# Compressed scores of both key groups by one block-diagonal product of 64 columns, issued in two halves between the last projections

## The reference, cut to what matters

```python
q_t = q.reshape(B, T, G, R, dh).transpose(0, 2, 3, 1, 4)       # dh = 64, T = 512
k_cmp = compress(kc, pe_k, w1k, w2k)                           # [B, 31, G, dh]
v_cmp = compress(vc, pe_v, w1v, w2v)
mask_c = cmp_end[None, :] <= t_idx[:, None]
s_c = jnp.einsum('bgrtd,bngd->bgrtn', q_t, k_cmp) * scale
p_c = masked_softmax(s_c, mask_c)
o_cmp = jnp.einsum('bgrtn,bngd->bgrtd', p_c, v_cmp)
...
o = g[..., 0:1] * o_cmp + g[..., 1:2] * o_slc + g[..., 2:3] * o_win
```

## Time and profile before

| what | value |
|---|---|
| median of 3 executions | 1792.61 us (1789.62 to 1793.20) |
| span of the profiled execution, first to last instruction | 1792.8 us |
| mean granted TensorE clock over the span | 0.994 of full |
| PE busy | 1768.5 us (99%) |
| POOL busy | 1180.3 us (66%) |
| DVE busy | 977.7 us (55%) |
| ACT busy | 382.7 us (21%) |
| the compressed scores on PE | 4.94 us, from 1236.35 us on |

### The profile page before, as it was taken

How to read it: one execution, slowest core, us unless ns; L and a number is a source line. 1 busy time by engine, 2 the same in 40 slices (tenths; PEclk the granted TensorE clock), 3 DMA queues, 4 the chain that set the end, 5 groups by cost and what they waited for, 6 DMA issues and landing times.

```text
span 1792.8 us, 24916 instructions
## 1 busy us (share of the span) xinstructions
PE 1768.5 (99%) x8821; PEld 1397.6 (78%) x8821; DVE 977.7 (55%) x1664; ACT 382.7 (21%) x827; POOL 1180.3 (66%) x1182
## 2 busy tenths in 40 slices
PE   8999999999999999999999999999999999999998
PEld 6888888888876788888888888878446778888887
DVE  4855345545664205465513556799874987007613
ACT  3111000012246311211100001454885110000001
POOL 4676677675665467667667668755754678668862
PEclk9999999999999999999999999999999999999999
DMA  9655465451330032455335543513000222332221
GB/s 355 216 189 172 141 212 189 150 155 62 104 94 24 24 101 92 160 170 187 123 109 190 187 129 94 127 50 95 25 24 1 94 71 94 110 100 92 97 94 47
DMA packets 245548, 212.93 MB, mean 119 GB/s; under 512 B 45985, under 2 KB 240990, under 8 KB 245470
## 3 DMA queue, kind: packets, MB, share of 16 engines
q1 hardware_dynamic: 229440, 211.18, 36.9%
q10 hardware_dynamic: 16030, 0.72, 0.5%
HBM read 209.72 MB, written 2.10 MB: 118 GB/s over the span
## 4 chain that ended last, share of the span: by engine, by line
PE 70%; POOL 13%; issue 9%; DVE 5%; DMA 1%; ACT 1%; ACTq 0%; POOLq 0%; DVEq 0%
PE ps L768 18%; PE ps L770 18%; PE ps L769 18%; POOL w_lo L697 8%; POOL w_hi L692 2%; PE ps L1376 2%; POOL w_hi L691 2%; PE ps L1387 2%; PE ps L1149 2%; PE ps L1407 2%; DMA raw<-in_ffn_w_down 1%; PE ps L1170 1%; PE ps L1158 1%; PE ps L809 1%; DVE tt L2258 0%
## 5 line engine op out<-in xcount | busy, mean ns | idle before, releaser
L697 POOL TENSOR_TENSOR w_lo<-raw,w_hi 128x512 fp32r<-128x512 f32 (+4 forms) x576 | 737.2, 1310 | 11.8
L768 PE MATMUL ps<-h_hi,w_hi 128*128 128x512 f32 x1192 | 468.1, 393 | 1.8 <-DVE h_lo L2540 1.4
L770 PE MATMUL ps<-h_hi,w_lo 128*128 128x512 f32 x1192 | 464.8, 390 | 0.0
L769 PE MATMUL ps<-h_lo,w_hi 128*128 128x512 f32 x1192 | 464.7, 390 | 0.0
L689 POOL TENSOR_TENSOR w_hi<-raw,ones 128x8 fp32r<-128x8 f32 x144 | 33.6, 233 | 450.0 <-PE ps L770 385.3
L768 PEld LDWEIGHTS ps<-h_hi,w_hi 128*128 128x128 f32 x1192 | 224.1, 188 | 54.4 <-issue 5.9
L770 PEld LDWEIGHTS ps<-h_hi,w_lo 128*128 128x128 f32 x1192 | 224.0, 188 | 47.5
L769 PEld LDWEIGHTS ps<-h_lo,w_hi 128*128 128x128 f32 x1192 | 224.1, 188 | 46.0
L768 PE MATMUL ps<-g_hi,w_hi 128*128 128x512 f32 x608 | 237.7, 391 | 0.1
L770 PE MATMUL ps<-g_hi,w_lo 128*128 128x512 f32 x608 | 236.6, 389 | 0.0
L769 PE MATMUL ps<-g_lo,w_hi 128*128 128x512 f32 x608 | 236.6, 389 | 0.0
(11 more groups left out here) (405 smaller groups left out, 2415.3 us busy)
## 6 DMA issues: line engine op xcount, KB each, us to landing
ada<-in_ada_w SPq DMA_DIRECT2D x31, 1024.0 KB, 7.0
ada<-in_w_ada SPq DMA_DIRECT2D x24, 1024.0 KB, 7.0
raw<-in_ffn_w_gate SPq DMA_DIRECT2D x22, 1024.0 KB, 5.2
raw<-in_ffn_w_up SPq DMA_DIRECT2D x22, 1024.0 KB, 5.1
raw<-in_w_in SPq DMA_DIRECT2D x16, 1024.0 KB, 5.1
raw<-in_w_up SPq DMA_DIRECT2D x16, 1024.0 KB, 5.3
raw<-in_w_down SPq DMA_DIRECT2D x16, 1024.0 KB, 4.7
raw<-in_ffn_w_down SPq DMA_DIRECT2D x16, 768.0 KB, 4.7
```

The lines of the kernel that those rows point to most:

```text
L697: last = pool.tensor_tensor(lo[:, c], src[:, c], hi[:, c].bitcast(F32), ALU.subtract)
L768: pe.matmul(o, wh, xh, start=start, stop=False)
L769: pe.matmul(o, wh, xl, start=False, stop=False)
L770: return pe.matmul(o, wl, xh, start=False, stop=stop)
```

## The change

The 32 score products of 64 rows by 32 columns (one for each head and each 128 tokens; the two groups in alternation, to banks 4 and 6) are replaced by 16 products of 128 rows by 64 columns: the queries of head hh of both groups, against a `kcmp` that is now zero outside its two diagonal blocks. Half of them (tokens 0 to 255) are issued in the middle of `proj(W_QD[1], 0)`, after `hidden_turn(1)`, to bank 4; the other half between `proj(W_QD[1], 0)` and `proj(W_QD[1], 1)`, to bank 6. Each half raises `cm_s` by one. `kcmp` is cleared once, early on DVE, and then filled by two copies of 64 x 32 in place of one of 128 x 64. `cmp_scores(b)` waits for its own half and reads it from one bank.

```diff
@@ -1356,16 +1356,23 @@
         proj(W_QD[0], 0, lambda: hidden_turn(0))
         proj(W_QD[0], 1, small_keys)
         compress(1)
-        pe.wait_ge(cm_kv_ev, 1)
-        for qc in range(NQ):
-            for h in range(NSA_HEADS):
-                gr, hh = h % 2, h // 2
-                last = pe.matmul(ps[:, 4 + 2 * gr, P * qc + 32 * hh:P * qc + 32 * hh + 32],
-                                 half_of(qn, gr, hh)[:, P * qc:P * qc + P],
-                                 half_of(kcmp, gr)[:, 32 * gr:32 * gr + 32], start=True, stop=True)
-        last.then_inc(cm_s, 1)
+
+        def compressed_scores(b):
+
+            pe.wait_ge(cm_kv_ev, 1)
+            for q in range(2):
+                for hh in range(NSA_HEADS // NSA_KV):
+                    first, col = P * (2 * b + q), 256 * q + 64 * hh
+                    last = pe.matmul(ps[:, 4 + 2 * b, col:col + 64], qn[:, hh, first:first + P], kcmp[:], start=True, stop=True)
+            last.then_inc(cm_s, 1)
+
+        def turn_and_scores():
+            hidden_turn(1)
+            compressed_scores(0)
+
         next_tile(W_QD[1])
-        proj(W_QD[1], 0, lambda: hidden_turn(1))
+        proj(W_QD[1], 0, turn_and_scores)
+        compressed_scores(1)
         proj(W_QD[1], 1, small_values)
@@ -2441,6 +2448,7 @@
         dve.wait_ge(nat_ev, NQ)
         step(dve.memset(v_diag[:], 0.0))
+        step(dve.memset(kcmp[:], 0.0))
         select(9)
@@ -2459,7 +2467,10 @@
         dve.wait_ge(cm_kv, 1)
-        dve.tensor_copy(kcmp[:], ps[:, 5, 0:64]).then_inc(cm_kv_ev, 1)
+        for gr in range(NSA_KV):
+            n = slice(32 * gr, 32 * gr + 32)
+            last = dve.tensor_copy(kcmp[HD * gr:HD * gr + HD, n], ps[HD * gr:HD * gr + HD, 5, n])
+        last.then_inc(cm_kv_ev, 1)
@@ -2469,11 +2480,11 @@
         def cmp_scores(b):
             s = cs[:, b]
-            dve.wait_ge(cm_s, 1)
+            dve.wait_ge(cm_s, b + 1)
             mask = kst[:, K_CADD + 64 * b:K_CADD + 64 * b + 64].rearrange("p (q n) -> p q n", n=32).unsqueeze(2).broadcast_to([P, 2, 4, 32])
             for gr in range(2):
                 ins = dve.tensor_tensor(s.rearrange("p (q g h n) -> p q g h n", q=2, g=2, n=32)[:, :, gr],
-                                        ps[:, 4 + 2 * gr, 256 * b:256 * b + 256].rearrange("p (q h n) -> p q h n", q=2, n=32),
+                                        ps[:, 4 + 2 * b].rearrange("p (q h g n) -> p q h g n", q=2, g=2, n=32)[:, :, :, gr],
                                         mask, ALU.add)
```

## The result

The changed kernel takes 1795.88 us in the median of 22 runs (1793.91 to 1801.38), the kernel before 1792.87 us in the same session. The ratio is 1.0019, with a 95% interval of 1.0013 to 1.0025: some 3.4 us slower, clear of noise, and just under the 0.2% at which the prediction drew its line. The forecast was 1794.0 us, within 1791.0 to 1797.0. The ratio leaves out two disturbed runs of the kernel before.

The account below looks back on a forecast made before the run. PE's chain was taken to bound this stage; -4.94 - 2.0 + 2.95 + 3.65 + 1.55 + 0.14 = +1.35 us at the last projection's end, +1.4 through DVE, gave 1794.0 us, range 1791.0 to 1797.0.

Parts of the forecast that it names:

- 2.95 us of waiting for POOL: PE after compress(1): idle until POOL's split of W_QD[1] ends, which the old scores had covered; +2.95 us.
- The chance for slower by more than 0.2%: Whole kernel above 1796.2 us: 0.12, from 0.06 of slower weight loads and 0.06 of scatter.
- The slow stretch: Projection products behind PE's new idle gap: half clock expected, +1.55 us, bounds 0 and 2.0.
- My other witness: Idle gap of 2.62 us on PE, one of two in the earlier trace read as followed by half clock.
- case 4: Clock does not recover before the new passes, which keep it low: another 1.55 us, 1795.6 us; chance 0.08.
- The old scores' slow stretch: Nine projection products behind the old scores at half clock; 2.0 us go away if those scores caused it.
- The new passes: The new scores on PE: 32 passes of 128 rows and 64 columns at 0.114 us each, +3.65 us.
- The lower bound for an old pass: Old score passes at full clock on PE: a start every 0.055 us, 3.5 us for all 64.
- The fill: Clearing kcmp early on DVE, on the chain to POOL's splits and PE: +0.14 us, or 0 if hidden.
- DVE's part: DVE behind the second half of scores: 3.44 us slack used up, rotation 13 and pair stage +1.4 us.
- rival 3: New passes do not overlap weight loads, 0.188 us each in place of 0.114: +2.4 us, 1796.4 us; chance 0.10.
- From span to median: Profiled span of 1792.8 us taken as 0.2 above the 1792.61 median; +1.4 us on that scale gives 1794.0.

Follow-up runs that it names:

- e3: The changed kernel with 12 idle 128x128 products put on PE into the gap where it waits for POOL; 1793.24 us, ratio 1.0002.
- e2: The kernel before, its 64 old passes issued in two halves at the changed kernel's places, DVE waiting for both halves; 1798.66 us, ratio 1.0037.
- e8: e1 with each of the 16 new products issued twice, 64 passes of 128 rows; 1792.78 us, ratio 1.0003.
- e6: The changed kernel, but DVE begins the first half of the scores only when both halves are there; 1797.57 us, ratio 1.0025.
- e5: The kernel before with 12 fills of kcmp on DVE where the changed kernel has one; 1796.29 us, ratio 1.0018.
- e1: The changed kernel's new products, but both halves at the old place, before the wait for the last projection tile; 1790.89 us, ratio 0.9989.

## Why the prediction was right, and where it was off

*Direction, mechanism and range* were right. The term that decided it, 2.95 us of waiting for POOL, was measured with 2.84 us of idle time, or 2.91 from start to start (1237.55 - 1234.43, less the 0.21 that stood between the last compression product and the scores before). The chance for slower by more than 0.2%, 0.12, was small for a result whose interval reaches 1.0025.

*The slow stretch was mis-sized.* The step reads: "The nearer of the two, with a full clock before it, cost 3.07 us at half clock". From the first product to the start of `hidden_turn` took 1242.83 - 1237.55 = 5.3 us; e3 has the same twelve in 2.85. With the beginning of the first scores it is 2.6 us: from the first product to the pair stage are 17.99 us in the changed kernel (1255.54 - 1237.55), and 15.37 in e3 at full clock. I had put 1.55, and an upper bound of 2.0, which the measurement passes. The kernel's own first gap had a longer stretch behind it than the one that I took.

*And the length is not the gap's alone.* In e2 the half clock behind the same wait held 3.4 us, about the length that I had taken. For the first block's gap, which is 2.02 to 2.03 us in every one of these traces, here is the same window in the kernel before, the changed kernel and e2:

```profile
535.00:542.50 7.50, 7.23 (x15) 3.92 (x16) 3.67 (x11) 4.03 (x10) 1.36 (x2) 0.54 0.20 69
535.00:542.50 7.50, 7.25 (x28) 4.46 (x30) 5.12 (x15) 4.93 (x13) 2.13 (x4) 0.77 0.19 67
535.00:542.50 7.50, 6.76 (x41) 4.20 (x42) 5.60 (x15) 5.81 (x16) 3.33 (x6) 1.00 0.23 81
```

The clock fell for 7 us, for 3.4, and not at all (nor in e8). So the rows of one trace could not give this term, neither its 1.55 nor the 2.62 with which I correct it: both are one execution's. The four traces with a gap of 2.84 to 2.99 us (changed, e6, e2, e5) all lost the clock, for 6.8, 6.8, 3.4 and 3.4 us. My other witness was weak, too: the gap of 2.62 us before the pair stage stands in e1 as well, where it ended at 1253.90 and the clock fell only at 1259.5.

*The second slow stretch as a rival* (case 4) is nearer in its size: it says another 1.55 on the forecast. The mechanism is another, though: the clock recovered inside the first half of the scores, at about 1243.3, so it was the stretch that was longer, not the new passes that held it low.

*The old scores' slow stretch*, 2.0 us, is right. From the start of the first product to the pair stage were 13.67 us before (1254.89 - 1241.22) and 11.73 in e1 (1249.77 - 1238.04): 1.94.

*The new passes*, 0.114 us each, cost 0.111 in the changed kernel's second half and in e8 (from 1233.32 to the next product at 1240.43, 7.11 us for 64). Inside the projections both halves add 3.64 us (e3's 15.37 less e1's 11.73), against 3.65 in the sum. The lower bound for an old pass, 0.055, was 0.066 in e2.

*The fill*, 0.14, cost 0 here, for the reason under e5.

*The sum again, with measured terms:* -4.94 - 1.94 + 2.91 + 3.64 + 2.62 = +2.29. From the fill of `v_diag` to the last product of the projections is +2.31 (89.56 against 87.25). Predicted was 1.35; the slow stretch accounts for the difference.

*DVE's part* was right in its form. I had the first maximum 4.7 us later; it came 5.7 later (94.69 us after the fill against 89.01), the extra microsecond being that of the clock. Its slack of 3.44 was used up, and rotation 13 ended 2.3 us later (98.16 against 95.85). e6 shows that this chain is the one that ends last.

*The weight loads* (rival 3, by the Trainium skill, "TensorE: Matmul & The Clock Gate", section "Part 3: Packing small matmuls — row/col tiling"): the passes of the changed kernel stand 0.111 us apart with loads of 0.192 in the median. The trace does not agree with the rule for these products, which fill all the rows.

*From span to median:* I read the span of 1792.8 as 0.2 above the median. Every run of the changed kernel has a time about 1.8 us above its span (1795.8 and 1794.0 for the profiled one). The profiled execution before was therefore, as an estimate from that, near 1794.6 us, some 2 us above the median, with more time at half clock. The prediction took a difference only, so it did not suffer; but it is why the two spans lie 1.2 apart and the runs some 3.

What stays open: what decides how long the half clock lasts behind a gap, and which length the timed runs had; and how far each part of the old passes' form, rows or columns, counts for the clock, since that was not separated. The form by itself at the new places (e2 against e6) rests on one trace each; the times leave it open.

## What to carry to other kernels

Before a piece of work is moved out of a place, ask what it covered there: here 4.9 us of small products hid 2.9 us of weight preparation. A gap on TensorE can cost twice: filling this one with useless products won back 2.6 us, and filling it with the new products themselves made the kernel faster than both. Halving the number of small matmuls is worth nothing like half of their time when the larger ones stand further apart, as here: 0.111 us for each in place of 0.066, so 3.6 us in place of 4.2. And a price of the clock that is read from one execution is one draw: look for the same gap in other traces before it goes into a sum.

## What the runs showed of the hardware that I had not expected

Passes of 64 rows and 32 columns, back to back with no gap, lost the full clock after 2.3 us, and again after 1.6 us in e5, while 64 passes of 128 rows and 64 columns held it through 7.1 us (e8), and so did 24 of 128x128 (e3). Gaps of 2.84 to 2.99 us were followed by half clock for 6.8 us in two traces and for 3.4 in two; one gap of 2.03 us was followed by 7 us, 3.4 us or none of it, by the execution. And a DVE instruction beside POOL's split ended 1.74 to 1.75 us after POOL's first instruction had begun, whether it started 0.21, 0.29 or 0.44 us after it, so that a small delay ahead of it vanished.
